# Block inverse of the gated delta rule: 64 of 128 columns in each product, read with a stride

## What is computed

```python
kk = jnp.einsum('bhnid,bhnjd->bhnij', kc, kc)
lower = jnp.eye(c, dtype=jnp.float32) + jnp.where(strict, bc[..., :, None] * kk * decay, 0.0)
rhs = jnp.concatenate([vc * bc[..., None], kc * (bc * jnp.exp(gam))[..., None]], axis=-1)
sol = lax.linalg.triangular_solve(lower, rhs, left_side=True, lower=True, unit_diagonal=True)
```

## Time and profile before

| what | value |
|---|---|
| median of 3 runs | 3359.6 us (3358.8 to 3359.79) |
| the profiled execution's own time | 3355.62 us |
| its span (first to last instruction) | 3353.6 us |
| PE busy | 3045.9 us, 91% of the span |
| VectorE busy | 2192.1 us, 65% |
| ScalarE busy | 1719.0 us, 51% |
| mean granted clock of PE | 0.949 of full speed |

### The profile page before, as it was taken

One profiled execution on the slowest core, in us unless ns is written; L12 is line 12 of the kernel. 1 busy time (PEld: TensorE's weight loads), 2 busy tenths in 40 slices (PEclk: granted clock), 3 DMA queues, 4 the chain that ended last, 5 costly groups with the idle time before them and its releaser, 6 DMA issues.

```text
span 3353.6 us, 65287 instructions
## 1 busy us (share of the span) xinstructions
PE 3045.9 (91%) x22954; PEld 2911.2 (87%) x22954; DVE 2192.1 (65%) x4518; ACT 1719.0 (51%) x3655; POOL 64.7 (2%) x113
## 2 busy tenths in 40 slices
PE   4977799989999999899989999998968589988898
PEld 4877699889999998799889999998958479976898
DVE  5649368777777774459777777777544348764586
ACT  1110256889844443556888944444432137462484
POOL 2200000000000000000000000000000000000000
PEclk9979899999999999899999999999978589997999
DMA  8940255434455553355344465554500035531453
GB/s 323 410 180 1 80 171 181 134 129 149 152 187 185 184 187 126 120 171 187 133 133 145 148 192 187 184 185 151 180 1 23 0 120 180 180 103 55 144 176 125
DMA packets 137757, 503.33 MB, mean 150 GB/s; under 512 B 15328, under 2 KB 15456, under 8 KB 137344
## 3 DMA queue, kind: packets, MB, share of 16 engines
q1 hardware_dynamic: 122544, 445.57, 40.2%
q0 software_dynamic: 15056, 55.65, 4.3%
HBM read 499.05 MB, written 2.10 MB: 149 GB/s over the span
## 4 chain that ended last, share of the span: by engine, by line
PE 69%; ACT 11%; DVE 7%; issue 2%; DVEq 1%; ACTq 0%
PE PB L483 9%; PE PB L485 9%; PE PB L484 9%; PE PA L485 9%; PE PA L483 8%; PE PA L484 8%; PE PB L473 4%; PE PA L659 3%; ACT onehot_a L1196 3%; ACT inv L1191 2%; ACT w_high L1019 2%; DVE w_low L1928 1%; PE PA L785 1%; PE PB L785 1%; DVE BIG L1954 1%
## 5 line engine op out<-in xcount | busy, mean ns | idle before, releaser
L1019 ACT ACTIVATE w_high<-ring 128x512 fp32r<-128x512 f32 x1484 | 915.1, 629 | 883.8 <-PE PA L485 472.3
L1928 DVE TENSOR_TENSOR w_low<-ring,w_high 128x512 fp32r<-128x512 f32 x1484 | 1009.2, 691 | 452.5 <-ACT w_high L1019 431.1
L483 PE MATMUL PB<-h_high,w_low 128*128 128x256 f32 x3536 | 1023.2, 289 | 48.6 <-DVE h_low L1616 36.5
L485 PE MATMUL PB<-h_high,w_high 128*128 128x256 f32 x3536 | 1003.2, 284 | 0.0
L484 PE MATMUL PB<-h_low,w_high 128*128 128x256 f32 x3536 | 1003.0, 284 | 0.0
L483 PEld LDWEIGHTS PB<-h_high,w_low 128*128 128x128 f32 x3536 | 685.6, 194 | 64.2 <-issue 39.4
L483 PE MATMUL PA<-a_high,w_low 128*128 128x256 f32 x2400 | 676.9, 282 | 5.0 <-DVE a_low L1937 5.0
L485 PE MATMUL PA<-a_high,w_high 128*128 128x256 f32 x2400 | 676.7, 282 | 0.0
L485 PEld LDWEIGHTS PB<-h_high,w_high 128*128 128x128 f32 x3536 | 675.5, 191 | 0.0
L484 PEld LDWEIGHTS PB<-h_low,w_high 128*128 128x128 f32 x3536 | 675.4, 191 | 0.0
L484 PE MATMUL PA<-a_low,w_high 128*128 128x256 f32 x2400 | 674.4, 281 | 0.0
(11 more groups left out here) (327 smaller groups left out, 2865.1 us busy)
## 6 DMA issues: line engine op xcount, KB each, us to landing
ring<-tiles SPq DMA_DIRECT2D x842, 512.0 KB, 3.3
BIG<-ada POOLq DMA_DIRECT2D x96, 512.0 KB, 14.1
BIG<-skew POOLq DMA_DIRECT2D x4, 512.0 KB, 4.3
X<-x SPq DMA_DIRECT2D x1, 1024.0 KB, 6.0
skew<-BIG POOLq DMA_DIRECT2D x1, 1024.0 KB, 7.0
out<-X SPq DMA_DIRECT2D x4, 256.0 KB, 2.0
con<-consts SPq DMA_DIRECT2D x1, 853.0 KB, 8.9
BIG<-masks POOLq DMA_DIRECT2D x1, 768.0 KB, 6.6
```

The lines of the kernel that those rows point to most:

```text
L483: mm(dst, lhs_l, high, start=start, stop=False, skip_group_check=True)
L485: return mm(dst, lhs_h, high, start=False, stop=stop, skip_group_check=True)
L1019: fn(tile_half(w_high, s, b), ring[:, at:at + HALF], ACT.Identity).then_inc(sem("high_ready"), 1)
L1928: tt(tile_half(w_low, s, b), ring[:, at:at + HALF], tile_half(w_high, s, b).bitcast(F32), ALU.subtract).then_inc(sem("low_ready"), 1)
```

## The change

In levels 1 to 6 each product computes only the 64 columns that can be other than zero. For c x and c^T y the moving operand is read out of the 128 columns with a stride, in runs of 2^lev columns. The results lie close together, 64 columns for a matrix, in PSUM; so do the copies `p1` and `p2`, which the second products read without a stride. The copies and the subtractions handle 384 columns for a group where it was 768. The subtractions write to `x` and `y` with the stride. The number of instructions, their order and their semaphores stay, and so do the stationary operands with their 128 columns.

```diff
+        HALF_COLS = P // 2
+
+        def of_half(x, lev, side):
+
+            return x.rearrange("p (m s l) -> p m s l", s=2, l=1 << lev)[:, :, side, :]
...
-                def times(dst, g, lhs, rhs):
+                def times(dst, g, lhs, rhs, lev=None, side=None):
+
                     for i in range(6 * g, 6 * g + 6):
-                        to = g * 1024 + (i % 6) * P
-                        ins = mm(dst[:, to:to + P], e[lhs][:, at(i)], e[rhs][:, at(i)], start=True, stop=True)
+                        to = g * 1024 + (i % 6) * HALF_COLS
+                        if lev is None:
+                            cols = e[rhs][:, i * HALF_COLS:(i + 1) * HALF_COLS]
+                        else:
+                            cols = of_half(e[rhs][:, at(i)], lev, side)
+                        ins = mm(dst[:, to:to + HALF_COLS], e[lhs][:, at(i)], cols, start=True, stop=True)
                     return ins
...
-                        times(PA, g, "ct", "x").then_inc(sem("inv_p1"), 1)
-                        times(PB, g, "c", "y").then_inc(sem("inv_p2"), 1)
+                        times(PA, g, "ct", "x", lev, 0).then_inc(sem("inv_p1"), 1)
+                        times(PB, g, "c", "y", lev, 1).then_inc(sem("inv_p2"), 1)
...
-                        part = slice(g * 6 * P, (g + 1) * 6 * P)
+                        part = slice(g * 6 * HALF_COLS, (g + 1) * 6 * HALF_COLS)
                         act.wait_ge(sem("inv_p1"), w.up(sem("inv_p1")))
-                        fn(e["p1"][:, part], PA[:, g * 1024:g * 1024 + 6 * P],
+                        fn(e["p1"][:, part], PA[:, g * 1024:g * 1024 + 6 * HALF_COLS],
                            ACT.Identity).then_inc(sem("inv_p1_ready"), 1)
                         act.wait_ge(sem("inv_p2"), w.up(sem("inv_p2")))
-                        fn(e["p2"][:, part], PB[:, g * 1024:g * 1024 + 6 * P],
+                        fn(e["p2"][:, part], PB[:, g * 1024:g * 1024 + 6 * HALF_COLS],
                            ACT.Identity).then_inc(sem("inv_p2_ready"), 1)
...
-                        part, src = slice(g * 6 * P, (g + 1) * 6 * P), slice(g * 1024, g * 1024 + 6 * P)
-                        tt(e["x"][:, part], e["x"][:, part], PA[:, src], ALU.subtract)
-                        tt(e["y"][:, part], e["y"][:, part], PB[:, src], ALU.subtract)\
+                        part, src = slice(g * 6 * P, (g + 1) * 6 * P), slice(g * 1024, g * 1024 + 6 * HALF_COLS)
+                        x, y = of_half(e["x"][:, part], lev, 0), of_half(e["y"][:, part], lev, 1)
+                        tt(x, x, PA[:, src].rearrange("p (m l) -> p m l", l=1 << lev), ALU.subtract)
+                        tt(y, y, PB[:, src].rearrange("p (m l) -> p m l", l=1 << lev), ALU.subtract)\
                             .then_inc(sem("inverse_step"), 1)
```

## The result

The changed kernel takes 3412.34 us (median of 4 runs, 3411.55 to 3418.93) against 3359.2 us (median of 4, 3356.9 to 3359.79): ratio 1.0164, 95% interval 1.0146 to 1.0181. It is slower by 53.1 us; +56.0 us was forecast. The profiled execution is the 3418.93 us one, with a span of 3417.0 us, and is the longest of the four; it reaches the inverse 8.5 us later than the kernel before, which the code ahead of the inverse, the same in both, cannot explain. So the stage is compared from its own start.

A forecast was written before the change was run, and what follows sets the result against it. PE bounds the inverse by loading 128 stationary columns per record, with the clock at 0.50 throughout. 55.9 - 0.8 + 0.9 = +56.0 us on the 3359.6 us median gave 3415.6 us; 8-in-10 range 3398 to 3422 us.

The forecast's parts named there:

- The record's price: PE's inverse records: 64 moving columns cost what 128 do, 0.112 us at the high clock, 0.213 us at the low.
- The clock: PE's clock in the inverse: stays at 0.50 through all 48 blocks; matmuls take 123.0 against 67.15 us, +55.9 us.
- The sum: Whole kernel: 55.9 for matmuls, -0.8 for the last subtractions, +0.9 for line 800, together +56.0 us.
- The last pair of subtractions: DVE at the end of the inverse: the pair takes 1.04 us instead of 1.83 us, -0.8 us.
- What lay behind the inverse: Three products after the inverse: line 800 goes from 2.00 to 2.94 us, +0.9 us; the other two stay at 2.94 us.
- The range for the clock edges behind the inverse: After the inverse: clock edges can fall otherwise, put at -1.5 to +1.5 us.
- The base: Kernel before: median 3359.6 us, 4.0 us above the profiled execution, carried along without a known reason.
- The clock did not rise by itself: Rival in the inverse: clock rises as before, only the end changes, -0.8 us, 3358.8 us; chance 0.10.
- not early and not late: Rival in the inverse: slow strided reads raise the clock after level 1 to 5, 3366 to 3405 us; chance 0.05.
- the stride is free: Strided moving reads in 144 of 288 matmuls: taken as 0; at half speed they would stay under the load.
- The faster rival: Inverse records' cost follows their columns, 0.059 us at the high clock; -33 us, 3327 us; chance 0.03.

The follow-up runs named there:

- first experiment: Level 1 put back to 128 columns in products, copies and subtractions, against the changed kernel; 3355.41 us, 0.9993 of the kernel before.
- level 4: Only level 4 put back to 128 columns, against the changed kernel; 3382.37 us, 1.0082 of the kernel before.
- the longer filler: Changed kernel plus 44 extra 128 x 128 matmuls on constants ahead of the inverse; 3347.76 us, 0.998 of the kernel before.
- third experiment: Changed kernel with one contiguous half of the columns read at every level, without the stride (wrong columns); 3411.55 us, 1.0165 of the kernel before.
- the filler of 36: 36 extra matmuls on constants ahead of the inverse: added to the changed kernel 3411.66 us, 1.0164; added to the kernel before 3353.34 us, 0.999.
- the narrow last level: Changed kernel with level 1 at 128 columns and level 6 with 64 stationary columns; 3347.55 us, 0.9973 of the kernel before.
- fourth experiment: Changed kernel with only the first 64 stationary columns per product, the other half of the result left out; 3321.04 us, 0.9891 of the kernel before.

## Why the prediction was right

- **The record's price.** "Below 128 columns it is not the stream that sets the distance" held: 0.111 us at the high clock with 64 columns (first experiment), 0.213 us at the low one. The cause, which the rows of before only suggested, is shown by halving the stationary operand: 0.058 and 0.107 us.
- **The clock.** The step that carried the forecast held: 0.50 through all 48 blocks. It was an extrapolation: it was taken from rows with 1 and 12 columns and from products with pauses, none of them with 64 columns, and that a 64-column stream would behave like these was an assumption that came out. The experiments with level 1, level 4 and the longer filler show it to be the whole of the loss.
- **The sum.** The inverse took 2633.14 - 2509.99 = 123.15 us against the 123.0 us of the forecast. The last pair of subtractions took 0.56 + 0.47 = 1.03 us where 1.04 us was expected.
- **What lay behind the inverse was mis-sized.** I had +0.9 us: line 800's records at the low clock, the other two products unchanged. In the profile the first of the three takes 2.94 us as said, with the clock at 0.50 to its end. The clock rises behind it, at about 2637.9 us, in the pause in which PE waits for the copy, and the other two take 1.62 us each instead of 2.94 us. That is 6.18 us against 7.88 us, -1.7 instead of +0.9. The outputs that follow run from 2644.02 to 2648.34, 4.3 us; in the kernel before they took from 2581.95 to 2587.84, 5.9 us, with the low clock up to 2585.2 us. Put together, from the start of the inverse: +56.0 for the inverse, -0.8 for the subtractions, -1.7 for the three products and -1.6 for the outputs, +51.9 us; 53.1 us was measured between the medians. The range for the clock edges behind the inverse, 1.5 us on either side, was too narrow.
- **Where the clock rises behind the inverse** is not fixed by the change. With the low clock up to the end of the inverse too, the third experiment's profile has these products at 2.94, 2.94 and 1.62 us, and that of the filler of 36 has all three at 2.94 us. Why the rise comes where it does stays open.
- **One reading of the rows was wrong.** Line 800's 2.00 us in the kernel before are not its time at the high clock. The clock was 1.00 up to 2571.5 us and 0.50 from 2572.0 us on, within those twelve records; at the high clock throughout they take 1.62 us (first experiment). The term of +0.9 us compares two measured times and stands as a difference.
- **The base.** I carried a gap of 4.0 us between the profiled execution and the median without a cause. The runs of the same kernel before lie between 3352.05 and 3363.49 us over the experiments, and the start of the inverse between 2499.9 and 2510.0 us in profiles with the same code ahead of it. The gap was within this scatter. Taking the median as the base was sound: the forecast of 3415.6 us lies 3.3 us above the measured 3412.34 us, 2.9 us of it by the sum (56.0 against 53.1) and 0.4 us by the median of the kernel before, which is 3359.2 us over its four runs.
- **The rivals.** The clock did not rise by itself, not early and not late, and the stride is free (third experiment). The faster rival's price of 0.059 us exists, but it belongs to the columns of the stationary operand and not to those of the moving one.

## What to carry to other kernels

Before halving the moving operand of small f32 products, see what sets the distance between records: where a load of 128 stationary columns stands for each one, half the columns are no time saved. Cutting the streamed work cost TensorE its high clock here, with PE still shown busy at 100%; so read the granted clock of the stage, and what the clock is when the stage is entered. If it falls, keep a first part at full width, or shorten the stationary operand where its other columns are not needed; here a full level 1 gave back the high clock, and the halved stationary operand of level 6 took another 5.7 us off the chain.

## What the hardware showed that I had not expected

- The 64-column stream did not raise the clock from 0.50 in 123 us, and did not lose one of 1.00 in 63.8 us. It kept what it found, but for the two runs with a pause of 1.4 us ahead of it, which lost the high clock 2 us later.
- 72 records of filler with that pause behind them changed nothing (1.0164), 88 records without it gave 0.998: 16 records of work without use are worth 62 us of an execution.
- The clock rises in the middle of a gapless stretch, after 63.6 us, once the columns per record double.
- Products in the two column halves of the array overlap at the change from one half to the other: a block of 12 records takes 0.52 us (2559.41 to 2559.93 in the timeline of the narrow last level) where blocks in one half take 0.70 us (fourth experiment). Alternating the halves within a block was not tried.
